# Seven block products in place of eight in the second feed-forward matrix, three rounds of four

## The reference, cut to what matters

```python
def _mlp(x, g, w_up, w_down):
    h = _rmsnorm(x, g)
    return jnp.square(jax.nn.relu(h @ w_up)) @ w_down
...
    x = x + _merge(conv_out, attn_out, gates, w_out)
    x = x + _mlp(x, g_mlp, w_up, w_down)
```

## Time and profile before

| | us |
|---|---|
| three runs | 953.61, 954.35, 953.61 (median 953.61) |
| the profiled execution's own time | 954.1 |
| its span, first to last instruction | 952.3 |
| PE busy in it | 941.3 (99%) |
| VectorE (DVE), ScalarE (ACT), GpSimd (POOL) busy | 535.3, 528.7, 257.3 |
| feed-forward part with the final norm, roughly | 561 to 952 |

### The profile page before, as it was taken

How to read it: one execution, slowest core, us unless ns; L and a number is a source line. 1 busy time by engine, 2 the same in 40 slices (tenths; PEclk the granted TensorE clock), 3 DMA queues, 4 the chain that set the end, 5 groups by cost and what they waited for, 6 DMA issues and landing times.

```text
span 952.3 us, 19721 instructions
## 1 busy us (share of the span) xinstructions
PE 941.3 (99%) x7473; PEld 923.1 (97%) x7473; DVE 535.3 (56%) x915; ACT 528.7 (56%) x826; POOL 257.3 (27%) x188
## 2 busy tenths in 40 slices
PE   8999999999999999999999999999999999999997
PEld 8899999999999999999999999999999999999997
DVE  6479999999999999997653322222111122221133
ACT  6788787878787878786733343333111133331153
POOL 5301010101010101012243444445334244454340
PEclk9999999999999999999999999999999999999999
DMA  6776667676758585768132223234233133243102
GB/s 181 151 175 132 171 125 176 121 180 116 185 109 184 109 181 113 158 144 211 46 110 80 80 85 101 85 93 120 89 88 89 47 88 88 88 121 98 45 23 95
DMA packets 189520, 111.37 MB, mean 117 GB/s; under 512 B 35437, under 2 KB 181277, under 8 KB 189482
## 3 DMA queue, kind: packets, MB, share of 16 engines
q1 hardware_dynamic: 176666, 80.28, 30.6%
q0 software_dynamic: 7632, 27.79, 15.9%
q10 hardware_dynamic: 5184, 2.78, 1.0%
HBM read 75.97 MB, written 7.06 MB: 87 GB/s over the span
## 4 chain that ended last, share of the span: by engine, by line
PE 97%; ACT 1%; DMA 1%; issue 1%; DVE 0%; POOL 0%; DVEq 0%; POOLq 0%
PE dense L551 83%; PE z L671 3%; PE dense L846 3%; PE z L635 2%; PE z L705 2%; DMA w_lo<-w_raw 1%; PE z L565 1%; PE z L639 1%; PE dense L715 0%; PE z L838 0%; PE z L629 0%; PE dense L578 0%; PE z L691 0%; PE z L710 0%; PE z L621 0%
## 5 line engine op out<-in xcount | busy, mean ns | idle before, releaser
L534 POOL TENSOR_TENSOR w_lo<-w_raw,w_hi 128x1024 fp32r<-128x1024 f32 x80 | 192.3, 2406 | 295.0 <-ACT w_hi L939 295.0
L551 PE MATMUL dense<-r_hi,w_hi 128*128 128x272 f32 (+1 forms) x1264 | 263.5, 291 | 1.2 <-DMA w_lo<-w_raw 0.6
L551 PE MATMUL dense<-r_lo,w_hi 128*128 128x272 f32 (+1 forms) x1264 | 262.6, 289 | 0.0
L551 PE MATMUL dense<-r_hi,w_lo 128*128 128x272 f32 (+1 forms) x1264 | 262.2, 289 | 0.0
L939 ACT ACTIVATE w_hi<-w_raw 128x1024 fp32r<-128x1024 f32 x134 | 140.9, 1054 | 113.6 <-PE dense L551 102.6
L551 PEld LDWEIGHTS dense<-r_hi,w_hi 128*128 128x128 f32 x1264 | 198.2, 188 | 1.6 <-DMA w_lo<-w_raw 0.8
L551 PEld LDWEIGHTS dense<-r_lo,w_hi 128*128 128x128 f32 x1264 | 198.8, 188 | 0.7 <-DVE r_lo L1355 0.6
L551 PEld LDWEIGHTS dense<-r_hi,w_lo 128*128 128x128 f32 x1264 | 199.1, 188 | 0.0
L1374 DVE SCALAR_TENSOR_TENSOR acc<-conv_in,cw_cur,acc 128x574 f32<-128x574 f32 x232 | 172.8, 811 | 0.5
L511 POOL DMA_DIRECT2D w_lo<-w_raw x53 | 45.2, 853 | 362.4 <-ACT w_lo L941 362.4
L551 PE MATMUL dense<-s_hi,w_hi 128*128 128x272 f32 x640 | 132.3, 288 | 0.0
(11 more groups left out here) (258 smaller groups left out, 1289.6 us busy)
## 6 DMA issues: line engine op xcount, KB each, us to landing
w_raw<-in_w_in_dram SPq DMA_DIRECT2D x54, 512.0 KB, 5.5
w_lo<-w_raw POOLq DMA_DIRECT2D x53, 512.0 KB, 5.0
w_raw<-in_w_up_dram SPq DMA_DIRECT2D x32, 512.0 KB, 4.0
w_raw<-in_w_down_dram SPq DMA_DIRECT2D x32, 512.0 KB, 3.5
w_raw<-in_w_pw_dram SPq DMA_DIRECT2D x8, 512.0 KB, 3.6
w_raw<-in_w_out_dram SPq DMA_DIRECT2D x8, 512.0 KB, 3.6
x_tok<-in_x_prompt_dram SPq DMA_DIRECT2D x4, 512.0 KB, 6.1
out_dram<-k_blk SPq DMA_DIRECT2D x32, 64.0 KB, 2.4
```

Of the source, the lines that this page charges most:

```text
L534: pool.tensor_tensor(w_lo[:, n], w_raw[:, n], w_hi[:, n].bitcast(F32), ALU.subtract).then_inc(lo_post, 1)
L551: mm = nc.tensor.matmul(out[:, h, 0:half], w[:, wslot, k, :], m[:, k, c0 + h * half:c0 + (h + 1) * half], start=(k == 0 and n == 0), stop= ...
```

## The change

The 16+16 units of a round become 8+8, in four rounds (`ROUNDS`, `up_group`). Rounds 0 to 2 make w_down's part with the Strassen-Winograd scheme, on pairs P of output tiles: the weights of a pair are a 2x2 matrix of blocks A (output tile 1 or 2; even or odd chunk k), each of 4 chunks x 128 columns, and the moving data a 2x2 matrix B (even or odd chunk; first or second 272 columns). Seven products of 12 matmuls (4 chunks m, three passes, 272 columns) stand in the place of eight: 84 matmuls of 272 columns for each pair where there were 96.

For this the weights need four sums (S1 to S4, each 128x512) beside three plain blocks, and the moving data four sums (T1 to T4) beside three plain ones:

- For each pair VectorE makes the four weight sums (`wsum_pair`), ScalarE seven high parts and GpSimd seven low parts, each 128x512 (`quarter_high`, `wsum_high`, `seven_low`). High and low places hold one pair: ScalarE may write a form's high part for the next pair once that product of this pair is done.
- For two tiles of w_up (a chunk pair m) VectorE makes four sums and seven low parts and ScalarE seven high parts, each 128x272 (`u_sum`, `u_low`, `u_sum_high`), in the place of two low and two high parts of 544 columns.
- VectorE adds the products to `xT` in nine additions of 272 columns with one input in PSUM (`add_product`) in the place of two of 544.

Round 3 stays with `unit` and `part_unit`. Order around the seams:

- VectorE makes the weight sums of a round's first pair behind `up` of f = 5, and those of each further pair within the additions of the pair before.
- ScalarE puts A11 and S1 between `up` of 5 and of 6; A12, S2, S4, S3 between `up` of 6 and of 7; A22 behind it.
- TensorE starts a round's seven products when both `dense` slots are emptied (`claim`), so once VectorE has taken unit f = 7 out of PSUM.
- Product S2 adds onto bank 0, where x11 was taken, so it waits for that addition; S3 waits for x12, A22 for z11.

```diff
+        SEVEN = (("A11", "B11", 0, True), ("S1", "T1", 1, True), ("A12", "B21", 2, True), ("S2", "T2", 0, False),
+                 ("S4", "B22", 3, True), ("S3", "T3", 0, False), ("A22", "T4", 2, True))
...
 @@ tensor
+            def seven(rr, p):
+                P_ = PAIRS * rr + p
+                if p == 0:
+                    for slot in range(2):
+                        claim(slot, X_EMPTIED[slot] + 2 * up_group(rr + 1))
+                if P_ >= 2:
+                    pe.wait_ge(product_added, N_ADDED * (P_ - 1))
+                for name, moving, b, begin in SEVEN:
+                    if name in QUARTER_FORMS:
+                        pe.wait_ge(quarter_lo[QUARTER_FORMS.index(name)], P_ + 1)
+                    else:
+                        pe.wait_ge(wsumlo_done, len(SUM_FORMS) * P_ + SUM_FORMS.index(name) + 1)
+                    before = {"S2": "x11", "S3": "x12", "A22": "z11"}.get(name)
+                    if before:
+                        pe.wait_ge(product_added, N_ADDED * P_ + ADDED[before])
+                    if p == 0 and name == "A11":
+                        pe.wait_ge(form_ready, form_count(rr, PAIRS - 2, U_FORMS[-1]))
+                    hi, lo = form_place(w_hi, name), form_place(w_lo, name)
+                    for m in range(PAIRS):
+                        if p == 0 and m == PAIRS - 1:
+                            pe.wait_ge(form_ready, form_count(rr, m, moving))
+                        for j, (w, low) in enumerate(((hi, False), (hi, True), (lo, False))):
+                            mm = nc.tensor.matmul(product_bank(P_, b), w[:, m, :], u_form(moving, m, low),
+                                                  start=(begin and m == 0 and j == 0), stop=(m == PAIRS - 1 and j == 2), skip_group_check=True)
+                    mm.then_inc(product_done, 1)
 @@ gpsimd
+            def seven_low(P_):
+                for name, _ in sorted(MADE.items(), key=lambda item: item[1]):
+                    if name in QUARTER_FORMS:
+                        f = QUARTER_FORMS.index(name)
+                        pool.wait_ge(quarter_hi, len(QUARTER_FORMS) * P_ + f + 1)
+                        pool.tensor_tensor(form_place(w_lo, name), quarter(P_, name), form_place(w_hi, name).bitcast(F32), ALU.subtract).then_inc(quarter_lo[f], 1)
...
 @@ scalar
+                high_post(g, 0)
+                up(g, rr, 4, 0)
+                high_post(g, 1)
+                up(g, rr, 5, 1)
+                if rr < N_SEVEN:
+                    quarter_high(P_, "A11")
+                    wsum_high(P_, "S1")
+                    up(g, rr, 6, 2)
+                    quarter_high(P_, "A12")
+                    wsum_high(P_, "S2")
+                    wsum_high(P_, "S4")
+                    wsum_high(P_, "S3")
+                    up(g, rr, 7, 3)
+                    quarter_high(P_, "A22")
+                    for p in range(1, PAIRS):
+                        seven_high(P_ + p)
 @@ vector, up(rr, f) behind the relu out of PSUM
+                dve.wait_ge(u32_done, KC * rr + f + 1)
+                if n % 2 == 0:
+                    u_sum(rr, m, "T1", b12, b11)
+                    u_low(rr, m, "B11", b11)
+                    u_low(rr, m, "T1", usum("T1"))
+                else:
+                    u_sum(rr, m, "T2", b22, usum("T1"))
+                    u_low(rr, m, "B21", b21)
+                    u_sum(rr, m, "T3", b22, b12)
+                    u_low(rr, m, "B22", b22)
+                    dve.wait_ge(usum_done, usum_count(rr, m, "T2"))
+                    u_sum(rr, m, "T4", usum("T2"), b21)
+                    for name in ("T2", "T3", "T4"):
+                        u_low(rr, m, name, usum(name))
...
+            def seven_added(P_):
...
+                made("A11")
+                add_product(P_, "x11")
+                following("S1")
+                following("S2")
+                made("A12")
+                add_product(P_, "z11", "x11")
+                following("S4")
+                made("S2")
+                add_product(P_, "x12")
+                add_product(P_, "y12", "x12")
+                following("S3")
...
+            for rr in range(ROUNDS):
+                for f in range(KC):
+                    up(rr, f)
+                    if rr < N_SEVEN and f == 5:
+                        for name in SUM_FORMS:
+                            wsum_pair(PAIRS * rr, name)
+                if rr < N_SEVEN:
+                    for p in range(PAIRS):
+                        seven_added(PAIRS * rr + p)
```

More of the change, by code:

```diff
@@ L313, in emptied_at, with form_place, quarter, wsum @@
             return X_EMPTIED[n % 2] + 2 * g + n // 2 + 1
+        FORM_HOME = {"A11": (0, 0), "A12": (0, 1), "S1": (1, 0), "S2": (1, 1), "S4": (2, 0), "S3": (2, 1), "A22": (3, 0)}
+        QUARTER_FORMS, SUM_FORMS = ("A11", "A12", "A22"), ("S1", "S2", "S4", "S3")
+        U_FORMS = ("B11", "T1", "B21", "B22", "T2", "T3", "T4")
+        U_SUMS = ("T1", "T2", "T3", "T4")
+        SEVEN = (("A11", "B11", 0, True), ("S1", "T1", 1, True), ("A12", "B21", 2, True), ("S2", "T2", 0, False),
+                 ("S4", "B22", 3, True), ("S3", "T3", 0, False), ("A22", "T4", 2, True))
+        MADE = {w: n + 1 for n, (w, _, _, _) in enumerate(SEVEN)}
+        ADDED = {"x11": 1, "z11": 2, "x12": 3, "y12": 4, "w12": 5, "x22": 6, "x21": 7, "y22": 8, "z21": 9}
+        N_ADDED = len(ADDED)
+        def form_place(buf, name):
+            slot, h = FORM_HOME[name]
+            return buf[:, slot, h * PAIRS:(h + 1) * PAIRS, :]
+        def quarter(P_, name):
+            slot = 2 * (P_ % 2) + (name[1] == "2")
+            return w_raw[:, slot].rearrange("p (k t) c -> p t k c", t=2)[:, int(name[2]) - 1]
+        def wsum(name):
+            at = OUTTOK + SUM_FORMS.index(name) * PAIRS * P
+            return gate_c[:].rearrange("p k c -> p (k c)")[:, at:at + PAIRS * P].rearrange("p (k c) -> p k c", c=P)
+        def usum(name):
+            at = U_SUMS.index(name) * HALFO
+            return part[:].rearrange("p n c -> p (n c)")[:, at:at + HALFO]
+        def u_form(name, m, low=False):
+            n = U_FORMS.index(name)
+            buf = ((r_hi, r_lo), (u_hi, u_lo))[n // 4][low]
+            return buf[:].rearrange("p k c -> p (k c)")[:, ((n % 4) * PAIRS + m) * HALFO:((n % 4) * PAIRS + m + 1) * HALFO]
+        def product_bank(P_, n):
+            return z[:, n, 0:HALFO] if P_ % 2 else dense[:, n % 2, n // 2, 0:HALFO]
+        def up_group(rr):
+            return 3 * GROUPS_PER_STAGE + GROUPS_PER_STAGE * rr
+        def form_count(rr, m, name):
+            return PRODUCTS * (PAIRS * rr + m) + U_FORMS.index(name) + 1
+        def usum_count(rr, m, name):
+            return len(U_SUMS) * (PAIRS * rr + m) + U_SUMS.index(name) + 1
         def psum2(slot, half):
@@ new lines, in _ @@
+            for rr in range(ROUNDS):
+                g0 = up_group(rr)
+                if rr > 0:
+                    pe.wait_ge(product_added, N_ADDED * (PAIRS * rr - 1))
+                with pe.Fori(g0 + 1 if rr == 0 else g0, g0 + 2) as g:
+                    group(g, s_hi, s_lo)
+                if rr < N_SEVEN:
+                    for p in range(PAIRS):
+                        seven(rr, p)
+            pe.wait_ge(product_added, N_ADDED * PAIRS * N_SEVEN)
+            for f in range(4):
+                unit(LAST_GROUP - 1, f, u_hi, u_lo, (u_ready, 1) if f == 0 else None)
+                if f >= 1:
+                    pe.wait_ge(xg_done, f)
+                    back(f - 1, ((0, 0), (1, 1), (2, 2), (3, 3)))
@@ L1213, in _, with up @@
             post(4, 6, out_squares)
[L1215 to L1217 removed]
+            def up(g, rr, f, n):
+                U = KC * rr + f
                 act.wait_ge(emptied[n % 2], emptied_at(g, n))
@@ L1226, in _, with seven_high @@
+            def seven_high(P_):
+                quarter_high(P_, "A11")
[5 more added lines that the diff above has]
+                quarter_high(P_, "A22")
+            for rr in range(ROUNDS):
+                g0 = up_group(rr)
                 if rr == 0:
@@ L1597, in up @@
[L1597 to L1600, removed]
-            dve.wait_ge(rstd_done, 2)
[L1603 to L1613, removed]
@@ new lines, in wsum_pair @@
+            def wsum_pair(P_, name):
+                if name == "S1":
+                    for slot in range(2 * (P_ % 2), 2 * (P_ % 2) + 2):
+                        dve.wait_ge(raw_seven[slot], 16 * (P_ // 2 + 1))
+                if P_:
+                    dve.wait_ge(wsumlo_done, len(SUM_FORMS) * (P_ - 1) + SUM_FORMS.index(name) + 1)
+                if name in ("S2", "S4"):
+                    dve.wait_ge(wsum_done, len(SUM_FORMS) * P_ + SUM_FORMS.index(name))
+                a, b, op = {"S1": (quarter(P_, "A21"), quarter(P_, "A22"), ALU.add), "S2": (wsum("S1"), quarter(P_, "A11"), ALU.subtract),
+                            "S4": (quarter(P_, "A12"), wsum("S2"), ALU.subtract), "S3": (quarter(P_, "A11"), quarter(P_, "A21"), ALU.subtract)}[name]
```

(12 more changed lines are left out.)

177 lines of the change are left out of this document (132 added, 45 removed).

## The result

| | median us | runs | ratio to before, 95% interval |
|---|---|---|---|
| before | 954.75 | 17 | |
| after | 956.62 | 17 | 1.0019 (1.0012 to 1.0026) |

The changed kernel is slower by 1.9 us, just under 0.2%. The kernel before gave 953.61 in the three runs known when the forecast was made and 954.75 in all 17 (one of them took 3262 us, which doesn't move the median), so 1.1 of the 2.6 us between 954 and 956.62 aren't the change's. 144 matmuls less are run, and all that they gave is lost at three places.

A forecast was written before the change was run, and what follows sets the result against it. TensorE, busy 99% of the span, was taken to bound the kernel. 17.2 us of removed matmuls against 17.5 of waits in three rounds gave +0.3, so 954 us; range 944 to 961, the forecast's own 952 to 958.5.

The forecast's parts named there:

- 0.79 us: TensorE's restart behind a wait: four matmuls took 0.79 us for 0.50 in the stream, so 0.29 beyond the wait.
- to 9.1: Round's seam, VectorE: four weight sums in turns with GpSimd's low parts run from 4.5 to 9.1 us.
- What is removed: w_down in three rounds: 1152 matmuls (143.7 us) become 1008 (126.5 us), 17.2 us less if TensorE never waits.
- GpSimd's 128x512: GpSimd's low part of one weight form: 1.29 us, with bounds 1.20 and 1.45.
- Port and turns: VectorE instructions with two SBUF inputs alternate with GpSimd's: 11.2 us of port a pair against 10.5 of TensorE.
- Rival 1: VectorE keeps the port when its instructions follow within 0.15 us: shorter seam waits, say 945 us; 15%.
- Rival 2: The port doesn't matter, only the wait for emptying f = 7 stays: 939.6 us; 5%.
- The seam's waits: Each round's first pair: TensorE waits 0.78 (emptying f = 7), 2.4 (x11), 1.8 us (x12); 5.8 with restarts.
- Later pairs: After a round's first pair: x12 comes some 7.3 us after the pair's start, S3 due at 7.5, no wait.
- rival 3: x12 0.4 us late in pairs 1 and 2 of each round, if GpSimd's low takes over 1.35: say 958.5 us, 26%.
- the clock: TensorE's granted clock over the whole changed part: stays at 1.00, no cost in the sum.
- Rival 4: Clock falls at the wait for x11, matmuls at half pace: 3 x 2.7 = 8 us more, 962 us; 4%.
- within 0.2%: Chance that the whole kernel's time lies within 1.9 us of no change: 24%; slower 46%, faster 30%.

The follow-up runs named there:

- experiments 1 and 2: Changed kernel, GpSimd's seven low parts per pair written by memsets that read nothing (8 of 64 columns; 16 of 32): 940.12 and 940.51 us.
- experiment 3: Changed kernel, in each round's first pair VectorE makes the next pair's four weight sums behind x12, not ahead of it: 953.49 us.
- 8 to 11: Changed kernel, queues reordered cumulatively (weight sums and high parts; first product's claim; x11 early; first sums split behind f = 4 and 5): 945.53, 943.80, 943.37, 941.74 us.
- experiment 6: Changed kernel, x11 of each round's first pair put ahead of the last three low parts of u of f = 7: 960.63 us.
- 10: Reordered kernel (earlier first sums, first product claiming only its own bank), with x11 of the first pair also made early: 943.37 us.
- experiments 4 and 5: Constant matmuls added before the first pair's waits for x11 and x12, in the changed kernel and in experiment 6's: 955.60 and 955.93 us.

## Why the prediction came out as it did

The time was forecast as 954 us, measured 956.62 (17 runs); the sum against before was +0.3, measured +1.9. Step by step (three of the forecast's terms don't come out as written, each by 0.2 us or less: "0.79 us" behind a wait is 0.77 by its rows, the weight sums "to 9.1" end at 8.9, and the list behind "some 7.3 us" adds up to 7.5, which is just when S3 is due):

- **What is removed**: right. 10.54 us a pair, where 10.5 was taken.
- **GpSimd's 128x512**: 1.28 us where 1.29 was taken; in turns 1.73, forecast up to 1.8. The bounds 1.20 and 1.45 fall. The weight sums have a mean of 1.27, where 1.4 was taken.
- **Port and turns**: right, and shown by experiments 1 and 2. VectorE's instruction of 272 columns took 1.52 beside a GpSimd instruction and 0.43 alone. Rival 1 (VectorE keeps the port) falls with the same rows: 705.90 and 707.35 both take 1.5, one after the other. Rival 2 would be 939.6, and with the order unchanged only the kernels in which GpSimd's seven low parts read nothing gave that (940.1, 940.5). The Trainium skill (SBUF — State Buffer, "Who interferes with whom") calls it an exclusive block; the trace agrees for each instruction, but neither engine keeps the port for long.
- **The seam's waits**: 0.78, 2.4, 1.8 forecast, 0.86, 2.39, 1.96 measured, in the places named (the last in round 0; in the others the clock had taken 1.5 of it). A restart cost 0.24 and not 0.29 (3.24 us for 24 matmuls that take 24 x 0.1255).
- **Later pairs, "no wait, by a hair"**: right in the kernel after. The hair was real (experiments 3, 8 to 11), so rival 3 is a matter of a few tenths that this kernel didn't use up.
- **The step that failed is the clock** (put at nothing in the sum). Rival 4 said that 2.8 us of idleness had been borne, that my longest wait with its restart was 2.7, and gave it 4% and 8 us. The first two numbers were right, but they are no bound: those 2.8 us were one idle stretch by itself, at the end. Here the clock fell at every seam with no wait over 2.4 us, each with one of 0.86 shortly before it. The size was wrong as well: 1.5 us and not 8, as each fall lasted 3.4 us at half pace and in two seams of three it lay ahead of the wait for x12, which it shortened. That two of three cost nothing is luck of the place: where nothing covers it (experiment 6) it is 4.7 us.

The forecast's share for "within 0.2%" and for "slower" meet at 1.9 us, and the kernel fell just there.

## What to carry to other kernels

When work moves from TensorE to engines with large reserves, look at what is queued ahead of each instruction that TensorE waits for, not at the sum of their loads: here 17 us of saved matmuls were lost or kept by the order of a few statements alone. On VectorE, count every instruction with two SBUF inputs as long as itself and a GpSimd instruction, wherever both are supplied, and put the additions from PSUM ahead of them, all that TensorE will wait for and not the first alone (experiments 6 and 10: what x11 gave, x12 took). And look at the granted clock at each new wait; a few matmuls on constants ahead of it show what the clock costs.

## What the runs showed of the hardware

- The granted clock fell from 1.00 to 0.50 behind waits of 0.86 and 2.4 us with 4.8 us of dense matmuls between them, for 3.4 us, and in one seam only behind a third wait of 1.96. It doesn't fall each time: in experiment 3 round 0 had the same two waits and no fall. With fillers of 0.22 us in the waits (the idle left is up to 1.2 us) it stayed at 1.00 in all three rounds of experiments 4 and 5.
- VectorE with two SBUF inputs and GpSimd reading SBUF take turns instruction by instruction (1.53 and 1.73 us, alone 0.43 and 1.28), though VectorE's next one starts 0.08 us before the one in front ends (705.90 + 1.53 against 707.35); the time waited is within the instruction's own duration in the profile, not in an idle time before it.
- GpSimd's memsets don't do this to VectorE: means of 0.44 and 0.68 us for 272 and 512 columns in the kernel with 1344 of them.
